# Two more experts' up weights loaded before the expert loop, the gate weights loaded at its end

## What is computed

```python
def swiglu(x, w13, w2):
    a, b = jnp.split(x @ w13, 2, axis=-1)
    return (jax.nn.silu(a) * b) @ w2
...
    y = swiglu(h, w_sh13, w_sh2)                      # shared expert
    for e in range(N_EXPERTS):                        # 64 experts, 8 chosen per token
        y = y + combine[:, e:e + 1] * swiglu(h, w_exp13[e], w_exp2[e])
...
        h = layer_norm(DN_ALPHA * h + moe(h, ...), ln2_g[i], ln2_b[i])
        pe = jnp.concatenate([p_prompt[i].reshape(B * S, PLE_DIM), p_sample[i].reshape(DB * T, PLE_DIM)], axis=0)
        h = h + jax.nn.sigmoid(h @ w_ple_gate[i]) * (pe @ w_ple_in[i])
```

## Time and profile before

| what | value |
|---|---|
| median of three runs | 1365.21 us |
| profiled execution, device time | 1366.66 us |
| its span, first to last instruction | 1365.0 us |
| PE busy | 1249.4 us (92%) |
| DVE busy | 676.8 us (50%) |
| granted TensorE clock, mean | 0.944 |
| moved by DMA | 317.41 MB, mean 233 GB/s |
| first up products of the expert loop | at 658.70 us |
| first addition of the last four results (L2347) | at 1274.31 us |

### The profile page before, as it was taken

How to read it: one execution, slowest core, us unless ns; L and a number is a source line. 1 busy time by engine, 2 the same in 40 slices (tenths; PEclk the granted TensorE clock), 3 DMA queues, 4 the chain that set the end, 5 groups by cost and what they waited for, 6 DMA issues and landing times. The chain is left out here.

```text
span 1365.0 us, 22791 instructions
## 1 busy us (share of the span) xinstructions
PE 1249.4 (92%) x7601; PEld 538.1 (39%) x7601; DVE 676.8 (50%) x1506; ACT 307.6 (23%) x586; POOL 429.5 (31%) x546
## 2 busy tenths in 40 slices
PE   5989989999997899999899998999999989996897
PEld 3455544445454544464322332222223323322343
DVE  1337828966885442584433344334343334326872
ACT  1027574543453200130011111111111101101211
POOL 4444528012332000101444443344433434330011
PEclk8988999999997799979999999999999989998899
DMA  8251220032112490222799999999999999999721
GB/s 254 65 160 48 66 93 6 0 123 71 46 44 62 156 349 2 81 113 96 263 380 413 416 415 418 403 411 410 406 404 401 410 388 404 413 387 359 269 62 38
DMA packets 92606, 317.41 MB, mean 233 GB/s; under 512 B 42361, under 2 KB 44061, under 8 KB 76152
## 3 DMA queue, kind: packets, MB, share of 16 engines
q1 hardware_dynamic: 68640, 268.58, 51.2%
q0 software_dynamic: 23904, 48.03, 9.7%
HBM read 298.62 MB, written 30.60 MB: 241 GB/s over the span
## 5 line engine op out<-in xcount | busy, mean ns | idle before, releaser
L1681 PE MATMUL ps<-arena 128*32 128x512 f32 x3072 | 360.8, 624 | 39.6 <-issue 23.3
L1002 POOL DMA_INDIRECT arena<-h_rows,arena x192 | 193.7, 1009 | 322.6 <-DVE arena L2181 270.1
L1681 PEld LDWEIGHTS ps<-arena 128*32 128x32 f32 x3072 | 104.4, 114 | 262.7 <-issue 260.3
L1073 ACT ACTIVATE arena<-ps 128x512 f32<-128x512 f32 (+9 forms) x270 | 122.0, 483 | 373.0 <-PE ps L1331 210.8
L1696 PE MATMUL ps<-arena 128*32 128x512 f32 x1536 | 173.9, 592 | 0.6 <-DVE arena L2230 0.6
L1357 PE MATMUL ps<-arena 128*128 128x512 f32 (+1 forms) x384 | 169.2, 596 | 5.6 <-DMA arena<-in_w_in 5.6
L2168 DVE TENSOR_SCALAR arena<-ps,arena 128x9 f32<-128x9 f32 x48 | 10.9, 227 | 223.2 <-DMA y_rows<-arena 186.0
L1357 PEld LDWEIGHTS ps<-arena 128*128 128x128 f32 x384 | 72.5, 193 | 94.5 <-issue 94.0
L1277 ACT ACTIVATE arena<-ps 128x256 f32<-128x256 f32 x48 | 18.4, 384 | 402.6 <-PE ps L1681 402.6
L1696 PEld LDWEIGHTS ps<-arena 128*32 128x32 f32 x1536 | 52.4, 110 | 112.5 <-issue 112.5
L1331 PE MATMUL ps<-arena 128*128 128x128 f32 (+2 forms) x471 | 69.4, 293 | 24.7 <-DMA arena<-in_x_prompt 8.7
(11 more groups left out here) (223 smaller groups left out, 1414.2 us busy)
## 6 DMA issues: line engine op xcount, KB each, us to landing
arena<-in_w_exp SPq DMA_DIRECT2D x64, 2048.0 KB, 16.3
arena<-in_w_exp SPq DMA_DIRECT2D x64, 1024.0 KB
arena<-in_w_in SPq DMA_DIRECT2D x6, 2048.0 KB, 11.0
arena<-y_rows SPq DMA_DIRECT2D x18, 512.0 KB, 13.1
arena<-y_rows SPq DMA_DIRECT2D x3, 2048.0 KB, 7.6
arena<-in_x_prompt SPq DMA_DIRECT2D x8, 512.0 KB, 6.4
arena<-in_w_out SPq DMA_DIRECT2D x2, 2048.0 KB, 14.6
arena<-in_w_ple_gate SPq DMA_DIRECT2D x1, 4096.0 KB, 14.8
```

The costliest lines, as they stand in the source:

```text
L1002: pool.indirect_dma_start(out=xg[k % 2][:, 256 * j:256 * j + 256], out_offset=None, in_=h_quarters, in_offset=bass.IndirectOffsetOnAxis(ap ...
L1073: return nc.scalar.activation(out, in_, ACT.Copy, scale=scale)
L1681: ins = mm(ps[k % 2][w, :], xgT[k % 2][:, kk, w], w13[c % 4][:, kk, :], start=(kk == 0), stop=(kk == KT - 1))
```

## The change

SP issues the up weights of expert 4 into ring 0 once the shared expert's up products are done, and those of expert 5 into ring 1 once its down products are done. PE takes experts 4 and 5 from there in the first eight experts. The first two groups of loads are written out: slots 0 and 1 get experts 8 and 9 where they got 4 and 5, and the second group loads nothing into them. From the third group on (experts 12 and up) the loads stand as before. The load of the gate weights moves from ahead of the expert loop to just ahead of `w_ple_in`, behind unit 8.

```diff
+        ahead = [r_.rearrange("p (k n) -> p k n", k=KT) for r_ in ring]
...
+        ahead_in = [sem("fifth_experts_up_weights_in"), sem("sixth_experts_up_weights_in")]
...
             def load_13(e, s, done=None):
-                sp.dma_start(w13_rows[s], a["w_exp13"][0][bass.ds(e, 1)]...
+                sp.dma_start(w13_rows[s] if s < 4 else ring[s - 4], a["w_exp13"][0][bass.ds(e, 1)]...
...
             for s in range(1, 4):
                 load_2(s, s)
+            filled(sp, ("s13", NT - 1))
+            load_13(4, 4, ahead_in[0])
             sp.wait_ge(h_stored, 16 * NT)
...
             load_13(3, 3)
             load_2(0, 0)
-            sp.wait_ge(sh_done, 1)
-            sp.dma_start(wpg, a["w_ple_gate"][0].rearrange("(k p) n -> p k n", p=P)).then_inc(fin_in, 16)
+            filled(sp, ("s2", NT - 1, 1))
+            load_13(5, 5, ahead_in[1])
+
             def load_four(g):
-                sp.wait_ge(up, 3 * g + 1)
-                load_13(4 * g + 4, 0)
-                if not isinstance(g, int):
+                if not isinstance(g, int) or g != 1:
+                    sp.wait_ge(up, 3 * g + 1)
+                    load_13(8 if isinstance(g, int) else 4 * g + 4, 0)
+                if not isinstance(g, int) or g != 0:
                     sp.wait_ge(down, 6 * g)
                     load_2(4 * g + 2, 2)
                     load_2(4 * g + 3, 3)
-                sp.wait_ge(up, 3 * g + 2)
-                load_13(4 * g + 5, 1)
+                if not isinstance(g, int) or g != 1:
+                    sp.wait_ge(up, 3 * g + 2)
+                    load_13(9 if isinstance(g, int) else 4 * g + 5, 1)
                 sp.wait_ge(down, 6 * g + 2)
...
             load_four(0)
-            with sp.Fori(1, NE // 4 - 1) as g:
+            load_four(1)
+            with sp.Fori(2, NE // 4 - 1) as g:
                 load_four(g)
...
             sp.wait_ge(up, last_round(NE - 3) + 1)
+            sp.dma_start(wpg, a["w_ple_gate"][0].rearrange("(k p) n -> p k n", p=P)).then_inc(fin_in, 16)
             sp.dma_start(wpin, a["w_ple_in"][0].rearrange("(k p) n -> p k n", p=P)).then_inc(fin_in, 16)
...
             def up_x(q, k):
                 i = UNROLL * q + k
+                first_eight = isinstance(q, int) and q == 0
                 for c in firsts(k):
-                    pe.wait_ge(w13_in[c % 4], 32 * q + 16 * (c // 4 + 1))
+                    if first_eight and c in (4, 5):
+                        pe.wait_ge(ahead_in[c - 4], 16)
+                    elif first_eight or c % 4 >= 2:
+                        pe.wait_ge(w13_in[c % 4], 32 * q + 16 * (c // 4 + 1))
+                    else:
+                        pe.wait_ge(w13_in[c % 4], 32 * q + 16 * (c // 4))
...
-                        ins = mm(ps[k % 2][w, :], xgT[k % 2][:, kk, w], w13[c % 4][:, kk, :], start=...
+                        ins = mm(..., (ahead[c - 4] if first_eight and c in (4, 5) else w13[c % 4])[:, kk, :], start=...
```

More of the change, by code:

```diff
@@ L767, in load_13 @@
             def load_13(e, s, done=None):
-                sp.dma_start(w13_rows[s], a["w_exp13"][0][bass.ds(e, 1)].rearrange("a (p j) n -> p (a j n)", p=P)).then_inc(done or w13_in[s], 16)
+                sp.dma_start(w13_rows[s] if s < 4 else ring[s - 4], a["w_exp13"][0][bass.ds(e, 1)].rearrange("a (p j) n -> p (a j n)", p=P)).then_inc(done or w13_in[s], 16)
             def load_2(e, s, done=None):
@@ L1680, in up_x @@
                         w = slice(32 * n, 32 * n + 32)
-                        ins = mm(ps[k % 2][w, :], xgT[k % 2][:, kk, w], w13[c % 4][:, kk, :], start=(kk == 0), stop=(kk == KT - 1))
+                        ins = mm(ps[k % 2][w, :], xgT[k % 2][:, kk, w], (ahead[c - 4] if first_eight and c in (4, 5) else w13[c % 4])[:, kk, :], start=(kk == 0), stop=(kk == KT - 1))
                 ins.then_inc(up, 1)
```

## The result

| | before | after |
|---|---|---|
| median of 13 runs each | 1365.21 us | 1370.36 us |
| ratio, 95% interval | | 1.0049, 1.0036 to 1.0063 |
| profiled execution, device time | 1366.66 us | 1370.53 us |
| its span | 1365.0 us | 1368.8 us |

The changed kernel is slower by 0.5% (5.15 us by the medians, 3.8 us between the two profiled executions). Eleven of its runs took 1369.0 to 1374.1 us and two 1379, at a mean granted clock of 0.937 and 0.939 as against 0.943 to 0.946; why, no run shows. In the changed kernel the up products are L1696, the scatter is L1019, DVE's first list step L2183, unit loads L833, unit additions L2333, the addition of the last four results L2362, the gate products L1843.

A forecast was written before the change was run, and what follows sets the result against it. The prediction took the expert loop and the first part of the tail to be bound by DMA bytes. Gate weights 10.1, less 0.5 of DMA slack, less 5.2 gained in the loop, gave +4.4 us: 1369.6 us, range 1361 to 1374.

The forecast's parts named there:

- Expert 4 free: Before the loop: expert 4's early load costs nothing, as DMA moves nothing from 622 to 637 us; otherwise 5.1 us.
- The gain of 5.2 us by round 6: First loop rounds: round 5's stall goes (4.3 us) and expert 10's backlog goes (0.9 us); later rounds run 5.2 us earlier.
- The gate weights, 10.1 us: Tail, behind unit 8: their 4.19 MB on full DMA delay units 9 to 19 by 10.1 us, range 3.0 to 13.0.
- The 90.7 us behind L2347: From the first addition of the last four results to the span's end: DVE and PE chain, unchanged at 90.7 us.
- the lasting lead: Loop: the two experts' whole lead of 10.1 us lasts and offsets the gate weights, about 1365.2 us; chance 0.14.
- the room in the tail: Tail: DMA has room, gate weights cost only 3.0 us; 1363.0 us, or 1358.1 with the whole lead kept; chance 0.17.
- the failed gain: Loop: round 5's stall stays or a later wait takes the gain back; +9.6 us, 1374.8, or 1377.7; chance 0.14.

The follow-up runs named there:

- the move alone: The kernel before with only the load of the gate weights moved to the end, experts 4 and 5 loaded as before: 1379.3 us, ratio 1.0081.
- gate weights in mid-loop: The changed kernel with the gate weights issued in the expert loop at the end of round 4, ahead of expert 8's down weights: 1363.11 us, ratio 0.9981.
- gate weights in halves: The changed kernel with half the gate weights issued in the first rounds after round 3, half behind the second tile's last choices: 1361.58 us, ratio 0.9969.
- no gate weights: The changed kernel without the load of the gate weights, 4.19 MB left out: 1360.52 us, ratio 0.9962.
- gate weights last: The changed kernel with the gate weights issued behind the last choices of the second tile, on their own semaphore: 1365.45 us, ratio 0.9992.
- with fillers: Unused matmuls in PE's wait for the first normed tile: kernel before, five 1365.94 us, three 1363.03; changed kernel with split gate weights, five 1359.76, three 1357.79.
- five fillers: The kernel before with five unused 128x512 matmuls in PE's wait for the first normed tile: 1365.94 us, ratio 1.0005.

## Why the prediction was right

Forecast were 1369.6 us and +4.4 us; measured are 1370.36 us, +5.15 by the medians and +3.8 between the profiled executions. The terms can be checked in the profiled executions alone.

- **Expert 4 free:** right; the load fell into an empty stretch.
- **The gain of 5.2 us by round 6:** right in place and nearly in size. From round 2 to round 6 the kernel before took 48.15 us, every kernel with the two experts ahead 43.91: 4.24 against 4.3. The other kernels without them took 48.1 to 49.7. The loop's later rounds are mostly 5.0 to 6.0 us earlier; at the last results it comes to 4.6 or 6.5 us, by the kernel that is taken as the measure. The reason was half right. It is the scatter on full DMA engines, as its landing shows. But I counted 6.29 MB that leave, gate weights among them, and the move alone shows that the 4.19 MB of the gate weights don't matter: what fills DMA at 694 us are expert loads that are issued just then, and the change takes experts 8 and 9 out of that stretch.
- **The gate weights, 10.1 us:** right in size. They cost 10.5 to 12.4 us at the last results (12.1 at unit 9). At unit 9 the tail's own rate, which I kept as the upper part of the range, was nearer than the row of the same transfer: 4.19 MB in 12.1 us are 347 GB/s. I had the units wait behind them in the queue. They wait ahead of it: SP issues unit 9 only at 1246.25, and the gate weights, issued at 1229.85 and landed in 17.7 us, are in at 1247.5. So whether a unit could overtake them isn't shown. The Trainium skill (page "DMA: Bandwidth & Descriptors", section "Queues, rings and completion order") says that descriptors are consumed in ring order on each DMA engine. The trace agrees for `w_ple_in`: issued at 1230.33 and landed in 19.4 us, it is in at 1249.7, behind the gate weights.
- **The 90.7 us behind L2347:** wrong by 2.2 us. I had named it as what would make the prediction wrong altogether. I had looked at PE's 2.90 us only as time in hand, not at the clock that PE has after it: 0.50 from 1285 to 1290 us in the kernel before, 1.00 after the change.

Terms by measurement: 10.5 - 4.6 - 2.2 = +3.7 (or 12.4 - 6.5 - 2.2). The first addition of the last results was forecast near 1278.7 and came at 1280.36, 1.7 us later; the missed 2.2 us behind it go the other way. So it is in part luck that the total lies this near. Of the rivals, the lasting lead is refuted by the loop's rounds, mostly 5 to 6 us earlier and not 10.1, and by the kernel with the gate weights in mid-loop; the room in the tail by unit 9; the failed gain by rounds 3 to 6.

## What to carry to other kernels

Where DMA is full up to the end of a stage, a load that is moved into it cost time wherever it stood (10.5 to 12.4 us ahead of the units, and 4.9 behind them, by the medians of the kernels with it there and without it); only where DMA idles was it free, and whether it idles is read from its share in short stretches, not from the engines. A place that looks like a collision (the gate weights at the loop's start) can be the free one: take the load away alone and see whether anything gets faster. And a short wait of PE ahead of a long chain of products is not harmless when the clock falls in it: look at the granted clock behind it.

## What was not expected of the hardware

In the kernel before, PE waited 2.90 us for the first normed tile and then ran at a granted clock of 0.50, 1.2 GHz, from 1285 to 1290 us. After a wait of 3.45 us (gate weights in halves) the products behind were slower as well, 15.42 us for 32, after 3.57 us (no gate weights) 17.00, and after 2.48 and 5.55 us (gate weights last) 15.65. With 1.29 us (after the change), 0.34 us or none (with fillers), the clock stayed at 1.00, 2.4 GHz, and they took 14.00. But the length of this wait doesn't decide it alone. With the gate weights in mid-loop (L1833, L1845) PE waited 1.69 us and the clock fell in the products, with the move alone (L1815, L1827) it waited 1.80 us and they took 14.00:

```profile
1283.48 1.06 PE L1833 MATMUL ps<-arena 128*128 128x128 f32 x8 [1.69 <-DVE arena L2087]
1285.28 17.07 PE L1845 MATMUL ps<-arena 128*128 128x512 f32 x32 [0.74 <-ACT arena L1084]
1285.00:1290.00 5.00, 4.72 (x6) 2.13 (x7) 4.83 (x7) 0.23 (x1) 0.00 (x0) 0.50 0.15 30
...
1299.78 1.06 PE L1815 MATMUL ps<-arena 128*128 128x128 f32 x8 [1.80 <-DVE arena L2069]
1301.58 14.00 PE L1827 MATMUL ps<-arena 128*128 128x512 f32 x32 [0.74 <-ACT arena L1072]
```

The change and the move alone are also the two kernels in which PE had waited over 15 us (15.17 and 15.44) ahead of the embeddings and had run at 0.50 behind that wait, from 1265 to 1270 and from 1275 to 1280 us. Whether that or the shorter wait kept the clock up later isn't shown; that unused matmuls in the wait kept it up is, in all four profiled executions with them. The clock is worth 2.2 us here, and it hid a third of what the change costs. One more difference has nothing to do with the change: the up products of round 1 took about 8.7 us in some profiled executions and 7.07 in others, with the experts loaded ahead or not. In the loop of the kernel before, nothing of it is left by round 6: it starts 71.54 us after the loop's first product with 8.77, and 71.34 (five fillers) with 7.07.
